# One inference step of a two-layer decoder on one core: sample latents earlier, their turnings inside an output buffer, and more unread products on TensorE

## The chip, the cores and the metric

The kernel runs on one NeuronCore of a Trainium2 chip. The metric is the device time of one launch in microseconds, the median of several runs; lower is better. TensorE (PE) multiplies matrices into PSUM, VectorE (DVE) and ScalarE (ACT) compute on what it leaves, GpSimd (POOL) and SyncE (SP) mostly issue transfers.

## The reference, cut to what matters

The program is one step of a decoder trunk with two layers, for a prompt of 512 tokens and for 8 sample requests of one token each, in float32. Layer 0 mixes tokens by sliding-window attention and retention, layer 1 by latent attention. Each layer then attends to 256 memory tokens and passes a mixture of 16 experts. The latent attention is the part in which work is moved:

```python
def mla_project(x, pos, w_in, q_norm, kv_norm, w_uq, w_uk):
    cq, ckv, kr = jnp.split(x @ w_in, [MLA_Q_RANK, MLA_Q_RANK + MLA_KV_RANK], axis=-1)
    ...
    q = (cq @ w_uq).reshape(B, S, MLA_HEADS, MLA_NOPE + MLA_ROPE)
    q_nope, q_rope = jnp.split(q, [MLA_NOPE], axis=-1)
    q_rope = rope(q_rope, pos)
    q_lat = jnp.einsum('bshn,chn->bshc', q_nope, w_uk)
```

The prompt's queries attend to 512 keys; the sample's `q_lat` and `q_rope` (8 requests, 8 heads) attend later to 1024 cached positions each, read from pages. After each memory attention a router picks two experts for each of the 520 tokens, and the tokens' rows are gathered by expert.

## The kernel before, in words

Every engine runs one program in an order written out by hand. PSUM is cut into four buffers of 1024 columns (two banks each). A list of jobs (`psum_jobs`) hands them out in turn: job n uses buffer n mod 4. `open_(key)` makes TensorE wait until job n-4, the last user of the buffer, has been released by the engine that read it; `close` tells the readers that the job is full; `taken(pe, key)` waits until a job's result has been copied out, that is for the same release. TensorE takes its instructions in order, so whatever is written behind a wait starts after it.

`unread_products(o, n)` is a helper of three lines: n float32 products of the identity with itself (128 columns) or with a constant (`routes`, 256 columns), into columns of an open buffer that nobody reads. The kernel before has 47 of them at seven places: ahead of the turning of a layer's last tile (4), around the last gated tile of retention (8 and 8), ahead of the first latent projection (6), and in the tables of the experts (2, 3, and 4 or 3).

The stages that the change touches, in order of time:

- Sliding attention. Block i is S (scores), T (the turning of the probabilities), O (the product with the values); between them stand projections of the input, `SWA_WEAVE`.
- Retention. For each tile n of 128 tokens: `retS` (scores), `retK` (keys turned), `retO` (output), `retU` (state), and the turning `retG` of the gated tile before. DVE multiplies `retS` by the decay and with that releases its buffer (line 2735).
- The state of the samples: `sU` (updates), `sO` (output), `sOt` (its turning), among the turnings `x.t` of tiles 0 to 3.
- The memory stage ends with the turnings `xm.t` of the normed tiles, the router's products `lg.t` (line 1579), and their turnings `rt` (lines 1590 and 1593). Tile 2's turning is copied by ACT alone, the others are shared by ACT (line 2109) and DVE (line 2896).
- The tables of the experts, in `experts`: `rank` (lines 1609 to 1616), `table` (1628 and 1634, twice: destinations, then gates), while DVE computes ranks and places in a chain of some fifty small instructions. DVE's line 3095 writes `block_tokens`, by which POOL gathers the rows of a block (line 883). `moeX` (line 1647) turns the gathered rows, `moeH` (1659) is the first product with an expert's weights.
- Latent attention. 16 blocks, in a software pipeline S.i+2, T.i, O.i-1 (lines 1928 and 1931; 1112; 1941). Between them stand `qn`, `qrope` (1892), `qrT` (1902, the turning of the rotary queries of a tile), `kn`, `vt` (1874, the values). Behind O.5 stand `ql` (line 1917, the sample's latents: 8 small products) and `qrT.4` (line 1905: the sample's rotary queries, 8 turnings of 8x8), each with a buffer of its own. ACT copies them out behind out.5.

Of the kernel before, what the change touches and what calls it, by code (L numbers as in the profile page):

```python
# [213 lines left out]
PAGE_DVE = keys("""pcT.0 pcT.2 pcT.4 max.0 pcT.7 scale.0 ga.2.0 ga.2.1 max.1 ga.3.0 scale.1 ga.3.1 ga.4.0 ga.4.1""")  # L214
SP_REQUESTS = 4

# [16 lines left out]
def block_order():  # L233

    out = [("X", 0), ("H", 0), ("X", 1)]
    for b in range(BLOCKS_M):
# [15 lines left out]
LATENT_BLOCKS_PE = keys("""qrope.0 kn.1 qrT.0 qn.2 qrope.1 S.0 qn.3 S.1 vt.0 qrT.1 S.2 T.0 qrope.2 S.3 T.1 O.0 vt.1 S.4 T.2 O.1 S.5 T.3 O.2  # L252
                        qrope.3 qrT.2 S.6 T.4 O.3 S.7 T.5 O.4 qrope.4 qrT.3 S.8 T.6 O.5 ql qrT.4 S.9 T.7 O.6 S.10 T.8 O.7 S.11 T.9 O.8
                        S.12 T.10 O.9 S.13 T.11 O.10 S.14 T.12 O.11 S.15 T.13 O.12 T.14 O.13 T.15 O.14 O.15""")
LATENT_BLOCKS_ACT = keys("""qn.1 kn.1 qrT.0 exp.0 qn.3 exp.1 vt.0 qrT.1 pT.0 exp.2 pT.1 out.0 exp.3 vt.1 pT.2 exp.4 out.1 pT.3 exp.5 out.2
                         qrT.2 pT.4 exp.6 out.3 pT.5 exp.7 out.4 qrT.3 pT.6 exp.8 out.5 ql qrS pT.7 exp.9 out.6 pT.8 exp.10 out.7
# [47 lines left out]
def decoder_step(nc, io, outs):  # L304
# [82 lines left out]
    with ExitStack() as ctx:  # L387
# [220 lines left out]
        def pair(key):  # L608
            return PS[:, J[key] % 4, :]
# [437 lines left out]
        def _(pe):  # L1047
# [15 lines left out]
            def transpose_x(i, t):  # L1063
# [4 lines left out]
                if i % 3 == 1 and t == NT - 1:  # L1068
                    unread_products(o[:, 896:1024], 4)
# [180 lines left out]
            def between(n):  # L1250
                for key in SWA_WEAVE[n]:
                    project(key)
# [72 lines left out]
            for n in range(4):  # L1325
# [7 lines left out]
                close(mm, key)  # L1333
                key = ("retK", n)
# [7 lines left out]
                o = open_(key)  # L1342
                taken(pe, ("retS", n))
# [50 lines left out]
            def state_output():  # L1394

                key = ("sO",)
                o = open_(key)
                taken(pe, ("sU", 3))
# [7 lines left out]
            def state_output_back():  # L1406

                key = ("sOt",)
                o = open_(key)
                taken(pe, ("sO",))  # L1410
# [42 lines left out]
            def memory_stage(l):  # L1453
# [116 lines left out]
                def logits(t):  # L1570
# [4 lines left out]
                    pe.wait_ge(s["wr_zero"], 1)  # L1575
                    taken(pe, ("xT", 3 * l + 1, t))
# [6 lines left out]
                def logits_back(t):  # L1583
                    key = ("rt", l)
                    o = open_(key) if t == 0 else pair(key)
                    if t == NT - 1:

                        taken(pe, ("xT", 3 * l + 1, t))
                        for k in range(KD):
                            pe.matmul(o[0:DB, t * 32:t * 32 + 20], xT[:, k, tile_cols(t)], wr[:, l, k, 0:20], start=(k == 0), stop=(k == KD - 1))  # L1590
                        return
                    taken(pe, ("lg", l, t))
# [11 lines left out]
            def experts(l):  # L1604
# [5 lines left out]
                unread_products(o[:, 768:1024], 2, routes)  # L1610
# [9 lines left out]
                unread_products(o[:, 768:1024], 3, routes)  # L1620
# [15 lines left out]
                block_sums(0, "dest_sums")  # L1636
                pe.wait_ge(s["dest_rows"], l + 1)
                block_table(0).then_inc(s["dest_table"], 1)
                pe.wait_ge(s["gates_ready"], l + 1)
# [40 lines left out]
                def step_x(b):  # L1680
                    key = ("moeX", l, b)
                    o = open_(key)
                    if b == 0:
                        unread_products(o[:, 768:1024], 3 if l else 4, routes)
# [3 lines left out]
                def step_h(b):  # L1688
# [4 lines left out]
                    else:  # L1693
                        pe.wait_ge(s["half_gained"], l + 1)
# [109 lines left out]
            def latent_blocks():  # L1804
# [91 lines left out]
                def q_rope_back(t):  # L1896
# [3 lines left out]
                    if t < 4:  # L1900
                        for c in range(2):
                            mm = pe.transpose(o[:, c * P:c * P + P], qr_tok[:, t % 2, c * P:c * P + P], ident[:, :])
                    else:
                        for h in range(8):
                            mm = pe.transpose(o[:, 8 * h:8 * h + 8], qr_rep[0:8, h, :], ident[0:8, 0:8])
# [29 lines left out]
                def apply(i, o, blk, v):  # L1935
                    n, h0, g, w = blk
                    taken(pe, ("vt", n // 2))
# [160 lines left out]
        def _(act):  # L2098
# [111 lines left out]
            def attention_steps(kind):  # L2210
# [19 lines left out]
                def outputs(i):  # L2230
                    n, h0, g, w = blocks[i]
                    if kind == "mla":
# [216 lines left out]
            def latent_attention():  # L2449
# [59 lines left out]
                def sample_turned():  # L2509
                    full(act, ("qrT", 4))  # L2510
                    for q in range(4):
# [855 lines left out]
```

## Time and profile before

| | us |
|---|---|
| median of 3 runs | 1015.01 (1011.78 to 1015.91) |
| the profiled execution | 1004.26 |
| its span, first to last instruction | 1002.5 |
| TensorE busy | 938.6 (94%) |
| VectorE busy | 511.1 (51%) |
| ScalarE busy | 354.1 (35%) |
| mean granted TensorE clock | 0.983 |

The profile is of one execution. "Busy" is time in which an engine ran an instruction, a share of the span. The granted clock is that of TensorE, 1.00 being 2.4 GHz and 0.50 being 1.2 GHz. In a row of the timeline, "x8" is the number of instructions that were merged, and the bracket is the idle time of the engine ahead of them and what ended it. A float32 product appears as two instructions.

### The profile page before, as it was taken

The numbers are of one execution on the slowest core, as the hardware profiler recorded it, in microseconds if no ns is written. First come the engines' busy times: TensorE is split into PE (matmuls) and PEld (weight loads), VectorE is DVE, ScalarE is ACT, GpSimd is POOL, SyncE is SP. The second block draws the span as 40 slices with busy tenths as digits, with TensorE's granted clock in tenths as the row PEclk, the third lists the DMA queues.
The fourth block names the chain that finished last, engine by engine and source line by source line (L and its number), as shares of the span: only waits on it lengthen the run. The fifth ranks groups of instructions, "written<-read, shape, count | busy, mean of one in ns | idle before, by whom it ended". The sixth has DMA issues, their size and how long they took to land.

```text
span 1002.5 us, 17774 instructions
## 1 busy us (share of the span) xinstructions
PE 938.6 (94%) x6956; PEld 570.4 (57%) x6956; DVE 511.1 (51%) x1068; ACT 354.1 (35%) x891; POOL 255.0 (25%) x307
## 2 busy tenths in 40 slices
PE   7998999999998998799999999999999979999995
PEld 6886787878544856533333666557558654333332
DVE  0236630366828758532222285775688783223237
ACT  3336442021002445133333364565215443333323
POOL 3650000051600002345420014550000025552130
PEclk9999999999999999799999999999999989999998
DMA  9827100272204472889999732460266177999977
GB/s 319 207 83 245 59 1 1 85 201 94 74 0 80 137 282 104 312 321 410 416 414 415 311 107 52 94 185 24 81 213 255 43 253 245 366 416 413 417 202 187
DMA packets 76268, 203.61 MB, mean 203 GB/s; under 512 B 18105, under 2 KB 42465, under 8 KB 67089
## 3 DMA queue, kind: packets, MB, share of 16 engines
q1 hardware_dynamic: 59264, 152.78, 41.6%
q0 software_dynamic: 16912, 49.59, 16.1%
q8 instruction: 60, 0.98, 0.4%
q14 instruction: 32, 0.25, 0.1%
HBM read 184.46 MB, written 25.92 MB: 210 GB/s over the span
## 4 chain that ended last, share of the span: by engine, by line
PE 70%; DVE 14%; DMA 9%; ACT 4%; issue 2%; POOL 1%; SPq 1%; DVEq 0%; POOLq 0%; ACTq 0%
PE PS L1659 15%; PE PS L1446 10%; PE PS L1089 8%; PE PS L1193 6%; PE PS L1676 6%; PE PS L1477 3%; DMA x<-y_tok 2%; PE PS L1647 2%; ACT arena L2100 2%; DMA ring<-in_moe_w_in_dram 2%; DMA arena<-in_moe_w_in_dram 2%; PE PS L1154 1%; PE PS L1112 1%; PE PS L1073 1%; DVE rowmax L2633 1%
## 5 line engine op out<-in xcount | busy, mean ns | idle before, releaser
L1659 PE MATMUL PS<-ring,arena 128*32 128x512 f32 x696 | 137.6, 592 | 1.0 <-DMA ring<-in_moe_w_in_dram 0.8
L2100 ACT ACTIVATE arena<-PS 32x520 f32<-32x520 f32 (+9 forms) x138 | 69.4, 515 | 161.7 <-PE PS L1089 39.3
L1659 PE MATMUL PS<-arena 128*32 128x512 f32 x600 | 106.8, 593 | 2.1 <-issue 2.1
L3182 DVE COPY arena<-PS 128x256 f32<-128x256 f32 x24 | 10.2, 425 | 174.0 <-PE PS L1667 174.0
L1089 PE MATMUL PS<-xT,ring 128*128 128x260 f32 x416 | 93.5, 385 | 4.8 <-DVE arena L2593 3.1
L1089 PEld LDWEIGHTS PS<-xT,ring 128*128 128x128 f32 x416 | 78.3, 190 | 19.1 <-DVE arena L2593 5.1
L2386 ACT ACTIVATE arena<-PS,lnc 128x128 f32<-128x128 f32 x184 | 66.9, 468 | 36.7 <-PE PS L1647 36.7
L1659 PEld LDWEIGHTS PS<-ring,arena 128*32 128x32 f32 x696 | 37.1, 110 | 55.5 <-issue 51.6
L1676 PE MATMUL PS<-ring,arena 128*32 128x512 f32 x408 | 65.4, 595 | 0.6 <-DVE arena L3182 0.6
L1193 PE MATMUL PS<-ring,xT 128*128 128x256 f32 (+2 forms) x336 | 65.2, 354 | 0.0
L887 POOL DMA_INDIRECT y_tok<-arena,slot_dest x22 | 22.3, 1014 | 167.4 <-ACT arena L2424 152.9
L849 POOL TENSOR_TENSOR rstd<-rstd,small 128x1 f32<-128x1 f32 (+1 forms) x20 | 13.5, 676 | 187.2 <-DVE rstd L2882 187.2
L1193 PEld LDWEIGHTS PS<-ring,xT 128*128 128x128 f32 (+1 forms) x336 | 57.0, 186 | 7.0 <-issue 0.2
L1446 PE MATMUL PS<-ring,xT 128*128 128x512 f32 x128 | 57.0, 593 | 0.0
L1659 PEld LDWEIGHTS PS<-arena 128*32 128x32 f32 x600 | 29.1, 110 | 47.9 <-issue 45.7
L2406 ACT ACTIVATE PS<-PS 128x256 f32<-128x256 f32 x24 | 8.8, 368 | 129.7 <-PE PS L1659 129.7
L2109 ACT ACTIVATE xT<-PS,lnc 128x128 f32<-128x128 f32 (+1 forms) x108 | 39.5, 450 | 36.9 <-PE PS L1073 19.2
L1676 PE MATMUL PS<-arena 128*32 128x512 f32 x216 | 50.8, 595 | 0.0
L2221 ACT ACTIVATE pbuf<-PS,negmax 128x256 f32<-128x256 f32 (+3 forms) x96 | 45.1, 480 | 16.1 <-DVE negmax L2640 15.9
L1659 PE MATMUL PS<-xT,arena 128*32 128x512 f32 x240 | 50.3, 592 | 0.0
L1446 PE MATMUL PS<-ring,arena 128*128 128x512 f32 x96 | 44.5, 599 | 0.5 <-DMA ring<-in_w_mem_o_dram 0.5
L1676 PE MATMUL PS<-xT,arena 128*32 128x512 f32 x144 | 43.5, 595 | 0.6 <-DVE arena L3182 0.6
(448 smaller groups left out, 1785.0 us busy)
## 6 DMA issues: line engine op xcount, KB each, us to landing
ring<-in_moe_w_in_dram SPq DMA_DIRECT2D x29, 1024.0 KB
arena<-in_moe_w_in_dram SPq DMA_DIRECT2D x25, 1024.0 KB
ring<-in_moe_w_out_dram SPq DMA_DIRECT2D x17, 1024.0 KB
ring<-in_w_in_even_dram SPq DMA_DIRECT2D x11, 1024.0 KB
xT<-in_moe_w_in_dram SPq DMA_DIRECT2D x10, 1024.0 KB
arena<-in_moe_w_out_dram SPq DMA_DIRECT2D x9, 1024.0 KB
xT<-in_moe_w_out_dram SPq DMA_DIRECT2D x6, 1024.0 KB
y_tok<-in_c_zeros_dram POOLq DMA_DIRECT2D x8, 512.0 KB, 11.2
```

Source lines behind the costliest of these rows:

```text
L887: pool.indirect_dma_start(y_tok[l][:, :], bass.IndirectOffsetOnAxis(ap=slot_dest[:, b:b + 1], axis=0), ybuf[:, buf, :], None, bounds_check ...
L1089: mm = pe.matmul(o[out_rows, 512 * h:512 * h + HALF], lhs(k), rhs(k)[:, HALF * h:HALF * h + HALF], start=(k == 0), stop=(k == nk - 1))
L1193: mm = pe.matmul(o[0:ROWS[t], n * width:n * width + width], xT[:, k, tile_cols(t)], w[:, k, cols], start=(k == 0), stop=(k == KD - 1))
L1446: mm = pe.matmul(o[0:ROWS[t], 512 * h:512 * h + 512], out_part(i, 2 * n + k, t), w[:, k, 512 * h:512 * h + 512], start=(n == 0 and k == 0) ...
L1477: mm = pe.matmul(o[:, j * r:j * r + r], w[:, k, j * P:j * P + P], xT[:, k, tile_cols(t)], start=(k == 0), stop=(k == KD - 1))
L1647: mm = pe.transpose(o[:, k * P:k * P + P], by_k[:, k, :], ident[:, :])
L1659: mm = pe.matmul(o[group(q), 0:512], xT_[:, k, group(q)], w(q, k), start=(k == 0), stop=(k == KD - 1), **quarter(q))
L1676: mm = pe.matmul(o[group(q), 512 * h:512 * h + 512], a[:, c, group(q)], w(q)[:, c, 512 * h:512 * h + 512], start=(c == 0), stop=(c == 1), ...
L2100: return act.activation(dst, src, ACT.Copy)
L2109: ins = act.activation(dst(k), src(k), ACT.Identity, scale=lnc[:, i, 0, k:k + 1], bias=lnc[:, i, 1, k:k + 1])
L2221: ins = act.activation(prob_view(kind, i)[:, h, :], score_view(kind, i)[:, h, :], ACT.Exp, bias=negmax[:, n % 2, h:h + 1], scale=SCALE[kin ...
L2386: ins = act.activation(dst[:, k, :], o[:, k * P:k * P + P], ACT.Identity, scale=lnc[:, 3 * l + 1, 0, k:k + 1], bias=lnc[:, 3 * l + 1, 1, k ...
```

## The change

Three things are done. In latent attention `ql` moves from behind O.5 to ahead of the second value product `vt.1` (on ACT: from behind out.5 to behind exp.3), and `qrT.4` loses its buffer: its eight turnings are made at the head of O.10, into the second bank of O.10's buffer, and ACT copies them with out.10. The job list is one shorter, so from `ql` on the jobs' buffers are other ones, and `vt.1` now waits for the release of S.3 where it waited for that of `qrope.2`. Third, unread products are added at these places:

| place | products added, columns | stands |
|---|---|---|
| x.1, x.2 of layer 0 | 2, 3 of 128 | behind open_, ahead of the norm's wait |
| sliding attention, ahead of qr.3 | 4 of 128 | ahead of open_ |
| retS 2 and 3 | 3, 3 of 128 | ahead of the next open_ |
| retO 0 | 5 of 128 | behind open_, ahead of taken(retS 0) |
| sO, sOt | 3, 2 of 128 | behind open_ |
| lg.1, both layers | 4 of 128 | behind open_ |
| rt, both layers | 2 of 128 | behind open_ |
| rank | 2 to 3 of 256 | ahead of the picks' wait |
| table | 3 to 6, and 1 and 1, of 256 | ahead of three waits |
| moeX 0 | 4 to 8 (layer 0), 3 to 6 (layer 1), of 256 | ahead of the gather's wait |
| moeH 0 | 1 of 256 | ahead of the gains' wait |

```diff
+TURN_UNREAD = {(0, 1): 2, (0, 2): 3, (1, NT - 1): 4, (4, NT - 1): 4}
+SAMPLE_TURNED = 10
-LATENT_BLOCKS_PE = ... T.1 O.0 vt.1 S.4 ... T.6 O.5 ql qrT.4 S.9 ...
+LATENT_BLOCKS_PE = ... T.1 O.0 ql vt.1 S.4 ... T.6 O.5 S.9 ...
-LATENT_BLOCKS_ACT = ... exp.3 vt.1 ... out.5 ql qrS pT.7 ...
+LATENT_BLOCKS_ACT = ... exp.3 ql vt.1 ... out.5 pT.7 ...
@@ transpose_x
-                if i % 3 == 1 and t == NT - 1:
-                    unread_products(o[:, 896:1024], 4)
+                unread_products(o[:, 896:1024], TURN_UNREAD.get((i, t), 0))
@@ between (sliding attention)
+                if n == 2:
+                    unread_products(pair(att_key("swa", "O", 0))[:, 896:1024], 4)
@@ retention, behind retS n
+                if n >= 2:
+                    unread_products(pair(("retG", n - 2))[:, 896:1024], 3)
@@ retO
                 o = open_(key)
+                if n == 0:
+                    unread_products(o[:, 896:1024], 5)
                 taken(pe, ("retS", n))
@@ sO
                 o = open_(key)
+                unread_products(o[:, 896:1024], 3)
                 taken(pe, ("sU", 3))
@@ sOt
                 o = open_(key)
+                unread_products(o[:, 896:1024], 2)
                 taken(pe, ("sO",))
@@ logits, logits_back
+                    if t == 1:
+                        unread_products(o[:, 896:1024], 4)
                     taken(pe, ("xT", 3 * l + 1, t))
...
+                    if t == 0:
+                        unread_products(o[:, 896:1024], 2)
                     taken(pe, ("lg", l, t))
@@ experts
-                unread_products(o[:, 768:1024], 2, routes)
+                unread_products(o[:, 768:1024], 3, routes)
                 pe.wait_ge(s["picks_ready"], l + 1)
...
-                unread_products(o[:, 768:1024], 3, routes)
+                unread_products(o[:, 768:1024], 6, routes)
...
                 block_sums(0, "dest_sums")
+                unread_products(o[:, 768:1024], 1, routes)
                 pe.wait_ge(s["dest_rows"], l + 1)
                 block_table(0).then_inc(s["dest_table"], 1)
+                unread_products(o[:, 768:1024], 1, routes)
                 pe.wait_ge(s["gates_ready"], l + 1)
...
-                        unread_products(o[:, 768:1024], 3 if l else 4, routes)
+                        unread_products(o[:, 768:1024], 6 if l else 8, routes)
                     pe.wait_ge(xs_in[b % 3], 16 * uses(BLOCKS_M, 3, l, b))
...
+                        unread_products(o[:, 768:1024], 1, routes)
                         pe.wait_ge(s["half_gained"], l + 1)
@@ apply (latent attention, TensorE)
+                    if i == SAMPLE_TURNED:
+                        pe.wait_ge(s["qrtok_ready"], NT)
+                        for h in range(8):
+                            pe.transpose(o[:, 512 + 8 * h:512 + 8 * h + 8], qr_rep[0:8, h, :], ident[0:8, 0:8])
@@ outputs (latent attention, ACT)
+                    if kind == "mla" and i == SAMPLE_TURNED:
+                        key = att_key(kind, "O", i)
+                        full(act, key)
+                        copy(oT[:, h0 // 2, tile_cols(n)], pair(key)[:, 0:P])
+                        for q in range(4):
+                            turned = pair(key)[32 * q:32 * q + 32, 512:576]
+                            ins = copy(qrS[32 * q:32 * q + 32, q, :, 0:8], turned.rearrange("p (h b) -> p b h", h=8))
+                        free(ins, key)
```

## Rows read from the trace of the kernel before

**Rows 1.** The page's chain of work that ended last, by engine.
```profile
PE 70%; DVE 14%; DMA 9%; ACT 4%; issue 2%; POOL 1%; SPq 1%; DVEq 0%; POOLq 0%; ACTq 0%
```
**Rows 2.** Windows: busy us of PE, PEld, DVE, ACT, POOL, granted clock, DMA share, GB/s.
```profile
405.20:418.90 13.70, 11.00 (x63) 7.88 (x62) 9.09 (x38) 0.87 (x4) 2.95 (x3) 0.50 0.83 292
...
687.50:695.40 7.90, 7.90 (x74) 7.81 (x72) 3.37 (x5) 4.27 (x5) 0.00 (x0) 1.00 0.01 2
```
**Rows 3.** Timeline of layer 0's router and tables: start, us, engine, line.
```profile
394.73 1.09 PE L1579 MATMUL PS<-xT,wr 128*32 128x128 f32 x32 [1.14 <-ACT xT L2109]
395.75 1.16 PE L1061 MATMUL PS<-ident 128*128 128x128 f32 x8
...
398.95 0.84 PE L1593 MATMUL PS<-small,sinf 128*128 128x20 f32 x6 [0.85 <-ACT xT L2109]
...
403.74 0.45 PE L1613 MATMUL PS<-arena,qdec 128*128 128x80 f32 x2 [1.40 <-DVE arena L3047]
...
404.84 2.43 PE L1061 MATMUL PS<-qdec,ident 128*128 128x256 f32 x6
...
408.58 1.79 PE L1628 MATMUL PS<-arena 128*32 128x128 f32 x20 [1.32 <-DVE arena L3075]
...
410.81 0.62 PE L1634 MATMUL PS<-small,arena 128*128 128x24 f32 x2 [0.43 <-ACT arena L2100]
...
411.86 0.16 DVE L3095 CAST block_tokens<-PS 128x12 uint32<-128x12 f32 x1
...
412.87 1.05 POOL L883 DMA_INDIRECT arena<-x_rows,block_tokens  x1 [12.56 <-DVE block_tokens L3095]
...
414.32 3.76 PE L1061 MATMUL PS<-qdec,ident 128*128 128x256 f32 x8
...
417.88 1.55 PE L1647 MATMUL PS<-ident,arena 128*128 128x128 f32 x8
...
424.15 0.97 PEld L1647 LDWEIGHTS PS<-ident,arena 128*128 128x128 f32 x8 [0.84 <-issue]
```
**Rows 4.** Timeline of layer 1, the first gather and what follows.
```profile
825.97 1.03 POOL L883 DMA_INDIRECT arena<-x_rows,block_tokens  x1 [12.61 <-DVE block_tokens L3095]
...
827.45 2.91 PE L1061 MATMUL PS<-qdec,ident 128*128 128x256 f32 x6
...
830.40 1.57 PEld L1647 LDWEIGHTS PS<-ident,arena 128*128 128x128 f32 x8 [0.76 <-DMA arena<-x_rows,block_tokens]
```
**Rows 5.** Timeline of retention.
```profile
212.26 1.23 DVE L2735 TENSOR_TENSOR arena<-PS,decay 128x1024 f32<-128x1024 f32 x1
213.63 1.97 PE L1346 MATMUL PS<-arena 128*128 128x64 f32 x16 [1.57 <-DVE arena L2735]
...
233.34 0.66 PE L1337 MATMUL PS<-ident,arena 128*128 128x128 f32 x4 [1.08 <-DVE arena L2778]
```
**Rows 6.** Timeline of the samples' state and the turnings of layer 0.
```profile
302.63 1.95 PE L1061 MATMUL PS<-ident 128*128 128x128 f32 x16
...
310.44 1.13 PE L1073 MATMUL PS<-ident,x 128*128 128x128 f32 x8 [1.09 <-DVE x L2888]
```
**Rows 7.** Timeline of sliding attention, ahead of qr.3.
```profile
89.21 7.28 PE L1089 MATMUL PS<-xT,ring 128*128 128x260 f32 x32 [1.87 <-DVE arena L2593]
```
**Rows 8.** Timeline of latent attention: vt.1, exp.3's end, ql, qrT.4, S.9, mask of S.14.
```profile
635.62 1.98 PE L1874 MATMUL PS<-ring,arena 128*128 128x512 f32 x4
...
636.94 0.20 ACT L2221 ACTIVATION_READ_ACCUMULATOR pbuf<-PS,negmax 128x1 f32 x1
...
653.12 1.06 PE L1917 MATMUL PS<-arena 64*128 64x8 f32 x16
...
655.02 0.66 PE L1905 MATMUL PS<-ident,arena 8*128 8x8 f32 x8 [0.83 <-ACT pbuf L2221]
655.60 0.92 PE L1928 MATMUL PS<-arena 64*128 64x384 f32 x4
...
675.06 0.43 DVE L2632 TENSOR_TENSOR PS<-PS,band 128x256 f32<-128x256 f32 x1
```

More of the change, by code:

```diff
@@ L251 @@
 LATENT_JOBS += [("oinT", 3), ("qn", 0), ("oinT", 4), ("kn", 0), ("qn", 1)]
-LATENT_BLOCKS_PE = keys("""qrope.0 kn.1 qrT.0 qn.2 qrope.1 S.0 qn.3 S.1 vt.0 qrT.1 S.2 T.0 qrope.2 S.3 T.1 O.0 vt.1 S.4 T.2 O.1 S.5 T.3 O.2
-                        qrope.3 qrT.2 S.6 T.4 O.3 S.7 T.5 O.4 qrope.4 qrT.3 S.8 T.6 O.5 ql qrT.4 S.9 T.7 O.6 S.10 T.8 O.7 S.11 T.9 O.8
+LATENT_BLOCKS_PE = keys("""qrope.0 kn.1 qrT.0 qn.2 qrope.1 S.0 qn.3 S.1 vt.0 qrT.1 S.2 T.0 qrope.2 S.3 T.1 O.0 ql vt.1 S.4 T.2 O.1 S.5 T.3 O.2
+                        qrope.3 qrT.2 S.6 T.4 O.3 S.7 T.5 O.4 qrope.4 qrT.3 S.8 T.6 O.5 S.9 T.7 O.6 S.10 T.8 O.7 S.11 T.9 O.8
                         S.12 T.10 O.9 S.13 T.11 O.10 S.14 T.12 O.11 S.15 T.13 O.12 T.14 O.13 T.15 O.14 O.15""")
-LATENT_BLOCKS_ACT = keys("""qn.1 kn.1 qrT.0 exp.0 qn.3 exp.1 vt.0 qrT.1 pT.0 exp.2 pT.1 out.0 exp.3 vt.1 pT.2 exp.4 out.1 pT.3 exp.5 out.2
-                         qrT.2 pT.4 exp.6 out.3 pT.5 exp.7 out.4 qrT.3 pT.6 exp.8 out.5 ql qrS pT.7 exp.9 out.6 pT.8 exp.10 out.7
+LATENT_BLOCKS_ACT = keys("""qn.1 kn.1 qrT.0 exp.0 qn.3 exp.1 vt.0 qrT.1 pT.0 exp.2 pT.1 out.0 exp.3 ql vt.1 pT.2 exp.4 out.1 pT.3 exp.5 out.2
+                         qrT.2 pT.4 exp.6 out.3 pT.5 exp.7 out.4 qrT.3 pT.6 exp.8 out.5 pT.7 exp.9 out.6 pT.8 exp.10 out.7
                          pT.9 exp.11 out.8 pT.10 exp.12 out.9 pT.11 exp.13 out.10 pT.12 exp.14 out.11 pT.13 exp.15 out.12 pT.14 out.13
@@ L1899, in q_rope_back @@
                     pe.wait_ge(s["qrtok_ready"], t + 1)
[L1900 to L1905, printed above, removed]
+                    for c in range(2):
+                        mm = pe.transpose(o[:, c * P:c * P + P], qr_tok[:, t % 2, c * P:c * P + P], ident[:, :])
                     close(mm, key)
@@ L2231, in outputs @@
                     n, h0, g, w = blocks[i]
-                    if kind == "mla":
+                    if kind == "mla" and i == SAMPLE_TURNED:
[6 more added lines that the diff above has]
+                        free(ins, key)
+                    elif kind == "mla":
                         take(att_key(kind, "O", i), oT[:, h0 // 2, tile_cols(n)], lambda o: o[:, 0:P])
@@ L2507, in sample_latents @@
                     free(ins, ("ql",))
-                def sample_turned():
-                    full(act, ("qrT", 4))
-                    for q in range(4):
-                        ins = copy(qrS[32 * q:32 * q + 32, q, :, 0:8], pair(("qrT", 4))[32 * q:32 * q + 32, 0:64].rearrange("p (h b) -> p b h", h=8))
-                    free(ins, ("qrT", 4))
                 exps, probs_turned, outputs = attention_steps("mla")
-                steps.update({"exp": exps, "pT": probs_turned, "out": outputs, "ql": sample_latents, "qrS": sample_turned})
+                steps.update({"exp": exps, "pT": probs_turned, "out": outputs, "ql": sample_latents})
                 for key in LATENT_BLOCKS_ACT:
```

## The prediction

> **What bounds the kernel now.** I read the chain of work that ended last first: 70% of it is TensorE, 14% DVE [rows 1]. So an instruction added to TensorE costs its whole length, unless it stands in a wait. Then I read the granted clock in windows. It is 1.00 nearly everywhere, but 0.50 (1.2 instead of 2.4 GHz) from 405.2 to 418.9 us, in the tables of layer 0, with TensorE busy 11.0 of 13.7 us [rows 2], and in a stretch as long at the same place of layer 1. TensorE had done little before either fall: in layer 0 it waited 1.40 us for the picks [rows 3]. In these stretches DVE's chain of small steps sets the pace, as the timeline shows: TensorE's waits end on DVE lines 3047 and 3075 [rows 3]. Last I read, for each place of the change, what ends the wait there, and whether the added products stand ahead of that wait or behind it.
>
> **Prices.** Eight unread products of 128 columns are busy 1.95 us [rows 6], four 1.16 [rows 3]: 0.20 us each at the full clock. Of 256 columns, four at half the clock take 3.76 [rows 3] and three 2.91 [rows 4]: 0.85 each, and 0.43 at the full clock.
>
> **The change part by part**, against the profiled execution.
>
> Sliding attention, four products ahead of the buffer wait of qr.3: 0.8 us in an idle time of 1.87 [rows 7]. Three behind retS 2 and 3, also ahead of the wait: 0.6 in 1.08 [rows 5], and the same at tile 3. Zero.
>
> retO 0, five products. They look as if they filled the 1.57 us ahead of line 1346 [rows 5]. But they stand behind `open_`, and the job list has retS 0, retK 0, two memory jobs, retO 0: the buffer that retO 0 opens is retS 0's, and is released by the same DVE instruction (line 2735) for which `taken` waits. The wait is over when they start. What follows is TensorE and DVE in turn (line 1346, the state, its copy on DVE, the next tile), with no slack: 5 x 0.20 = +1.0 us. Bounds: 0 if something unseen were late as well, 1.2 at the price of the row with four.
>
> Samples' state. sO is the same trap: its buffer is sU 3's, for which it also waits. Three products behind that wait, then three ahead of x.2's norm, make 1.2 us, of which the idle time of 1.09 ahead of x.2 [rows 6] hides all but +0.1. The two of sOt and the two of x.1 lie in waits of their own. Bounds: 0, and 2.0 if all ten were on the path.
>
> lg.1, both layers. Its idle time of 1.14 ends with ACT line 2109 [rows 3], the copy of tile 2's turning, which frees the very buffer that lg.1 opens. The four products come behind it, 0.8 us. They push the four products and the turning of tile 4 by about 0.5, but what is waited for next (398.95, again ACT's copies, of tile 3) does not depend on them: I take 0, at most 0.4 a layer. rt, both layers: its buffer is freed by that last copy too, so its two products (0.4) come after the wait of 0.85 [rows 3], and the router's turnings, DVE's whole chain and the gather behind them start 0.4 later. That is +0.4 in each layer, counted in the next part.
>
> Tables, if the clock stays up. The third rank product (0.43) fits in the 1.40 ahead of the picks. The table's six (2.6 us, from 404.84+0.4) end at 407.8, ahead of the places (408.58+0.4). The one before L1634 (0.43) lies in a wait of 0.43; line 3095, which releases the gather, comes at its turn on DVE, which is busy till then. So the gather starts at 412.87+0.4 [rows 3]. In layer 1 it took 830.40-825.97 = 4.43 us to the turning that waited for it [rows 4]; in layer 0 this gives 417.3, and 417.7 after. Before, TensorE was still busy with the four slow products and turned at 417.88 [rows 3]. Eight at the full clock are 3.4 us from about 414.0: 417.4, in time. The turnings of the first half take 0.3 less (weight loads 1.57 at half the clock [rows 4], 0.97 at the full [rows 3], half of the difference). Layer 0: -0.2-0.3 = -0.5, rt's 0.4 inside. Layer 1 waited for the gather before, so +0.4-0.3 = +0.1. The product ahead of moeH (0.43) lies in a wait of about 1 us.
>
> Latent attention. Behind O.5, ql takes TensorE from 653.12, then qrT.4 waits 0.83 us for exp.8, turns, and S.9 starts at 655.60 [rows 8]. Without both S.9 could start at 653.1: -2.5. But ahead of vt.1 (635.62) ql costs its 1.0, and vt.1's buffer is now S.3's, released when exp.3 has ended, at 636.94+0.20 = 637.14 [rows 8]: vt.1 starts at 637.2, +1.6 in all (ql hides in it). All that follows to S.8 hangs on S and exp by turns, so S.9 gains 2.5-1.6 = 0.9. T.7 then waits some 0.2 for exp.8. The eight turnings in O.10 (0.6, [rows 8]) meet DVE, which takes S.14's mask at 675.06, half a us after its scores end: +0.1. ACT has the four copies in its wait for T.12. Together -0.6. Bounds: -1.6 if vt.1 didn't wait, +0.6 if nothing at S.9 came back.
>
> Sum: +1.0 +0.1 -0.5 +0.1 -0.6 = +0.1 us. The profiled execution took 1004.26 (span 1002.5 and 1.8 around it), the median of the runs is 1015.01, 10.8 above it. No step of the sum depends on what makes that difference, so I carry the +0.1 over: 1015.1.
>
> **The rule weighed against the trace.** From 687.5 to 695.4 TensorE ran turnings, nearly all 64 of them without a gap, and the clock stayed 1.00 [rows 2]. The Trainium skill, "TensorE: Matmul & The Clock Gate", section "Part 4: PE-mode transpose", says that a transpose does not count as activity for the clock. By that rule the turnings ahead of moeH would not bring it back; by the row they do. The row decides.
>
> **Rivals.**
> (a) The clock falls in spite of the products. Then the table's six take 5.1 us, end at 410.4, 1.4 after the places; the product before L1634 costs 0.85 instead of 0.43; the gather leaves 1.1 later than with the clock up; and the eight ahead of moeX run from 416.2, slow till 418.9 and fast from there, to 420.9 where 417.88 was: +3.1-0.3 = +2.8 in layer 0. Layer 1 with six, by the same steps, +2.5. With the rest: +1.1-0.6+5.3 = +5.8, 1020.8. It decides at the products behind 404.84: as soon as those start slow. For it: the stretch of the tables has few real products. Against it: the stretch before the fall now holds three products more, and rt's are moved into it.
> (b) The low clock costs half its length. If all work in the two low stretches were on TensorE's path, half of its busy 11.0 us would come back, twice: -11, and 1004. Against it: DVE is busy 9.1 of those 13.7 us [rows 2], and TensorE's waits end on it. The skill's page named above, section "Terms", counts the penalty as throttled time x (1-K/N), which is 13.7 us for the two stretches and would give 1001; the rows on DVE speak against it.
> (c) The timed executions lie 10.8 us above the profiled one, and a part of that may be low clock at waits where this execution kept it, in retention or the router, with long product runs behind. If the products at those waits hold it, -6: 1009. Nothing in this trace shows it; only the distance speaks for it.
> (d) The products behind waits are all on the path: 5+10 in layer 0's first half, 6 and 6 around the routers, 27 x 0.20 = 5.4, where the sum has 1.9; with latent attention at its upper bound (+0.6) and the tables as forecast without rt's part (-1.2) that is +4.8: 1020.
> (e) The change does nothing: the clock falls as before, with the long waits hiding all the products. 1015.
>
> **How the numbers follow.** About 0.5% (5 us) is what a measurement of this kernel tells from no change. Forecast 0.52, (a) 0.14, (b) 0.07, (c) 0.14, (d) 0.07, (e) 0.06. Slower by over 0.5%: most of (a) and (d), 0.18. Faster: (b) and most of (c), 0.20. The rest, 0.62, is within. The likeliest case alone has 1012 to 1018; the range reaches 1009 of (c) and 1020.8 of (a): 1008 to 1021.
>
> **What would show it.** After: a granted clock of 1.00 through both tables (wrong: 0.50 there, with the six products at 0.85 each). Line 1346 of tile 0 about 1.1 us behind DVE's line 2735 instead of 0.1. rt's two products between ACT's copy and line 1593, with 0.4 us more. moeX 0 of layer 0 waiting for the gather. vt.1 with an idle time ended by ACT, S.9 right behind O.5. The prediction is wrong if the clock falls in the tables, if the gain of latent attention is above 1.6 or below zero, or if the span moves by more than 5 us.

## The result and the profile after

| | before | after |
|---|---|---|
| median, us | 1012.31 (10 runs, 1006.43 to 1017.01) | 1007.21 (10 runs, 1002.71 to 1009.71) |
| ratio, 95% interval | | 0.9944 (0.9921 to 0.9967) |
| profiled execution, us (span) | 1004.26 (1002.5) | 1005.44 (1003.7) |
| mean granted clock of it | 0.983 | 0.994 |

The change is worth 0.56%, where no move was forecast. The ratios, here and below, are of fast executions alone. Against the forecast of 1015.1 the median is 7.9 us lower, of which 2.7 are the base: the kernel before has a median of 1012.31 over these ten runs, where the three runs of the prediction had 1015.01. The two profiled executions say the opposite: the one of after is 1.2 us longer. That is no contradiction, but the point of this case. The profiled execution of before, on which the whole prediction rests, was one of its luckiest: of 104 further executions of that kernel three took 1004.3 or less, and their mean was 1013.1.

First, the two profiles against each other. The busy line and the chain of after:

```profile
PE 951.3 (95%) x7072; PEld 580.4 (58%) x7072; DVE 511.1 (51%) x1068; ACT 354.0 (35%) x891; POOL 254.8 (25%) x307
...
PE 74%; DVE 12%; ACT 6%; DMA 5%; issue 2%; POOL 1%; SPq 0%; DVEq 0%; POOLq 0%; ACTq 0%
```

TensorE's share of the chain has grown from 70% [rows 1], and the unread products of 128 columns (line 1063) are now among its lines, with 1%. Windows of after (length, then busy us of PE, PEld, DVE, ACT, POOL with counts, granted clock, DMA share, GB/s): the tables of layer 0, the stretch at vt.1, the stretch behind O.5, and one at 705 us.

```profile
399.00:418.00 19.00, 15.93 (x140) 12.46 (x140) 14.99 (x65) 2.88 (x11) 5.04 (x7) 1.00 0.86 302
637.20:640.60 3.40, 3.40 (x7) 0.84 (x5) 0.00 (x0) 1.01 (x1) 2.14 (x4) 0.50 0.43 99
...
656.00:680.00 24.00, 23.87 (x172) 12.51 (x168) 19.05 (x44) 15.99 (x45) 11.28 (x21) 1.00 0.59 195
705.40:708.90 3.50, 3.50 (x53) 2.32 (x48) 1.14 (x1) 0.00 (x0) 0.00 (x0) 0.51 0.00 0
```

The tables keep 1.00 where they had 0.50 [rows 2]. Two short stretches at 0.50 are new against the first profile, at vt.1 and at 705 us.

Retention, TensorE of after (start, us, engine, line; the bracket is the idle time ahead and what ended it). The wait of 1.48 ends with DVE's line 2753 (2735 before), and only then do the five products run. Line 1353 (1346 before) starts 1.2 us behind its old place [rows 5]:

```profile
213.71 1.38 PE L1063 MATMUL PS<-ident 128*128 128x128 f32 x10 [1.48 <-DVE arena L2753]
214.93 1.90 PE L1353 MATMUL PS<-arena 128*128 128x64 f32 x16
```

The router and the tables of layer 0, same columns. The six products of the table take 2.79 and end ahead of the places. The eight ahead of moeX 0 take 3.70 and the turnings (line 1662, 1647 before) start 0.5 later than before [rows 3]. But this execution came 0.8 late to lg.1 (395.50 against 394.73) and lost 0.55 more at rt (400.27 against 398.95, less those 0.8). It is 1.3 late there and 0.5 late at the turnings, so the tables gave back 0.8. lg.1's own four products took 1.1; the wait of 0.85 that stood ahead of rt, now gone, hides them:

```profile
395.50 1.16 PE L1063 MATMUL PS<-ident 128*128 128x128 f32 x8 [1.12 <-ACT xT L2125]
396.59 1.09 PE L1590 MATMUL PS<-xT,wr 128*32 128x128 f32 x32
...
399.73 0.71 PE L1063 MATMUL PS<-ident 128*128 128x128 f32 x4
400.27 0.74 PE L1606 MATMUL PS<-small,sinf 128*128 128x20 f32 x6
...
406.07 2.79 PE L1063 MATMUL PS<-qdec,ident 128*128 128x256 f32 x12
409.81 1.36 PE L1641 MATMUL PS<-arena 128*32 128x128 f32 x20 [0.95 <-DVE arena L3093]
...
414.70 3.70 PE L1063 MATMUL PS<-qdec,ident 128*128 128x256 f32 x16
418.39 1.16 PE L1662 MATMUL PS<-ident,arena 128*128 128x128 f32 x8
```

Latent attention, TensorE of after: ql (line 1929), a wait of 0.52 for exp.3 as worked out, then vt.1, which takes 3.10 instead of 1.98 [rows 8] as the clock falls under it; further on, S.9 (line 1940) right behind the work of O.5, where ql, the wait and qrT.4 stood:

```profile
634.87 1.06 PE L1929 MATMUL PS<-arena 64*128 64x8 f32 x16
636.45 3.10 PE L1890 MATMUL PS<-ring,arena 128*128 128x512 f32 x4 [0.52 <-ACT pbuf L2237]
639.48 1.22 PE L1940 MATMUL PS<-arena 64*128 64x256 f32 x4
...
654.97 0.66 PE L1957 MATMUL PS<-pT,xT 128*64 128x128 f32 x8
655.56 0.92 PE L1940 MATMUL PS<-arena 64*128 64x384 f32 x4
```

Every local step is there, and the span moved by 1.2 us where 0.1 was forecast. So the 5 us must come from executions that look different. The theory that the experiments test, the **clock theory** (rival (c), widened): in other executions of the kernel before the clock falls in more places, with work behind them that TensorE bounds, and the change prevents that. Its rival, the **order theory**: the gain is the new order of the work (the wait behind O.5 gone), and the profiled pair hides it by chance. In the texts recorded before the first four runs they are called theory 1 and theory 2; theory 3 there is that transfers make the executions differ.

### The profile page after: what moved, and what is told of

Its sections match the earlier page's. It is cut to its first block, busy times and chain, and to the rows that moved or that the text cites. A ratio compares the mean times of both kernels' runs of the same rounds, so it can differ in the third digit from the quotient of the medians.

```text
span 1003.7 us, 17995 instructions
## 1 busy us (share of the span) xinstructions
PE 951.3 (95%) x7072; PEld 580.4 (58%) x7072; DVE 511.1 (51%) x1068; ACT 354.0 (35%) x891; POOL 254.8 (25%) x307
## 4 chain that ended last, share of the span: by engine, by line
PE 74%; DVE 12%; ACT 6%; DMA 5%; issue 2%; POOL 1%; SPq 0%; DVEq 0%; POOLq 0%; ACTq 0%
PE PS L1674 16%; PE PS L1455 10%; PE PS L1090 8%; PE PS L1691 8%; PE PS L1194 6%; PE PS L1486 3%; DMA x<-y_tok 2%; PE PS L1662 2%; ACT arena L2116 2%; PE PS L1113 2%; PE PS L1155 1%; PE PS L1063 1%; ACT xT L2125 1%; PE PS L1074 1%; DMA ring<-in_w_in_even_dram 1%
## 5 line engine op out<-in xcount | busy, mean ns | idle before, releaser
L3200 DVE COPY arena<-PS 128x256 f32<-128x256 f32 x24 | 10.2, 425 | 172.9 <-PE PS L1682 172.9
```

## The experiments

Each timed kernel ran 12 times. They ran in three groups (the first four, the next four, the last four of the table), each with its own 34 or 35 runs of the kernel before. "Clock lost" is (1 - mean granted clock) x span, averaged over the runs: the full-speed time that the low clock took away, if all of it were on the path. It is not: in each of the 18 profiles 2.3 to 4.0 us of it stand behind the last product, where TensorE has nothing left to do (the window below is the end of before's first profile). The ratio stands with its 95% interval; it is not the quotient of the two medians of all runs. Beside it stands the ratio of the plain means of the same executions.

```profile
995.80:1002.50 6.70, 0.00 (x0) 0.00 (x0) 4.10 (x7) 1.54 (x3) 0.00 (x0) 0.50 0.40 157
```

| kernel | median, us | range | ratio | by means | clock lost, us |
|---|---|---|---|---|---|
| before, all three groups | 1013.2 | 1002.5 to 1023.2 | | | 28.9 |
| b_again (before, unedited) | 1014.50 | 1006.8 to 1020.5 | 0.9997 (0.9961 to 1.0032) | 1.0004 | 29.8 |
| products_only | 1011.40 | 1006.9 to 1015.7 | 0.9970 (0.9941 to 0.9999) | 0.9984 | 11.5 |
| move_only | 1009.01 | 1003.9 to 1018.2 | 0.9934 (0.9897 to 0.9972) | 0.9960 | 24.9 |
| tables_only | 1011.33 | 1005.6 to 1018.0 | 0.9988 (0.9953 to 1.0024) | 0.9988 | 17.0 |
| turn_only | 1010.30 | 1007.6 to 1018.9 | 0.9984 (0.9956 to 1.0012) | 0.9984 | 27.6 |
| ql_only | 1013.83 | 1006.6 to 1022.2 | 1.0007 (0.9977 to 1.0037) | 0.9999 | 29.1 |
| turn_filled | 1009.02 | 1006.4 to 1018.2 | 0.9979 (0.9951 to 1.0007) | 0.9973 | 24.0 |
| front_only | 1013.06 | 1009.1 to 1023.0 | 1.0022 (0.9991 to 1.0053) | 1.0005 | 26.7 |
| after_again (the changed kernel) | 1006.07 | 1002.6 to 1009.8 | 0.9960 (0.9927 to 0.9992) | 0.9948 | 7.3 |
| freed | 1005.38 | 1001.6 to 1010.0 | 0.9942 (0.9913 to 0.9971) | 0.9936 | 6.3 |
| freed_vt | 1004.22 | 1000.3 to 1006.8 | 0.9918 (0.9890 to 0.9947) | 0.9918 | 5.7 |
| move_vt | 1006.70 | 1002.9 to 1014.4 | 0.9966 (0.9935 to 0.9997) | 0.9960 | 22.6 |

(One run of before at 5371 us and one of turn_filled at 3317 us are left out.) Over the 104 runs of before, an execution's time rises by 0.91 us with each us of clock lost, from 986.9 at none (correlation 0.91). What makes executions of this kernel differ goes with the clock; theory 3, by which the clock would be the same in all of them, falls with that. The line is not one for other kernels: after_again lost 7.3 us of clock, where it reads 993.5, and its mean was 1006.5.

### Where the low clock lies: six profiles of the kernel before

The unedited kernel was run once more in the first group, and four times later for its profile alone.

> The kernel before, once more, without any edit. Theory 1 (the gain of the change is low clock avoided: the one profiled execution of before, 1004.3, was its fastest, and its typical execution, 1012, loses more to a low clock): its executions spread over some 10 us, and their mean granted clock falls as their time rises, from about 0.983 at 1004 to about 0.975 at 1014. Theory 2 (the gain is the order of the work in latent attention) and theory 3 (the spread is transfers): the clock is 0.983 in all of them, whatever the time. The ratio to before should be 1.000, which also shows how well five rounds tell kernels apart.

> The kernel before, unedited; this run and the next three are for their profiles. Fixed places: low clock recurs at 214 to 225 us (price 4.2) and behind O.5, 655 to 679 us (price 5 to 7), each in 1 to 3 of the four, and always in both tables; an execution's time is 1004.3 plus the prices of its stretches, to 2 us. Spread loss: low stretches elsewhere, outside those two places and the tables, make up more than half of the time above 1004.3.

> As before_1: tables low; retention and O.5 low or not, with 4.2 and 5 to 7 us where low.

> As before_1: tables low; retention and O.5 low or not, with 4.2 and 5 to 7 us where low.

> As before_1: tables low; retention and O.5 low or not, with 4.2 and 5 to 7 us where low.

b_again's executions spread over 14 us, with the clock falling faster than I expected: about 0.970 at 1014 us, where I had 0.975. Its profiled execution took 1020.23, 16 us more than the one the prediction used, with the same instructions in the same order. Two of its low stretches, as windows:

```profile
214.40:224.60 10.20, 10.20 (x45) 9.30 (x45) 5.48 (x9) 0.00 (x0) 5.05 (x8) 0.50 1.04 214
...
664.90:678.60 13.70, 13.53 (x56) 6.80 (x56) 4.75 (x12) 5.41 (x21) 8.24 (x17) 0.50 0.45 101
```

In both TensorE is busy nearly all the time and DVE 54% and 35% of it: here TensorE sets the pace, which it did not in the tables [rows 2]. The second begins behind ql, the wait and the turnings of qrT.4. TensorE of b_again:

```profile
663.18 1.06 PE L1917 MATMUL PS<-arena 64*128 64x8 f32 x16
665.07 1.02 PE L1905 MATMUL PS<-ident,arena 8*128 8x8 f32 x8 [0.83 <-ACT pbuf L2221]
666.02 1.65 PE L1928 MATMUL PS<-arena 64*128 64x384 f32 x4
```

The same four instructions of S.9 took 0.92 in [rows 8].

To see what each stretch costs, I matched DVE's instructions of two profiles one by one and took how far one runs behind the other at fixed points. The differences from point to point (points in us of before's first profile, rounded; the last column closes the sum to the span) give the time gained or lost in each section against that first profile:

| profile (span) | to 203 | retention, to 232 | samples' state, memory attention, to 380 | router, tables, to 440 | experts, to 600 | latent, to 680 | to 850 | to the end |
|---|---|---|---|---|---|---|---|---|
| b_again (1018.5) | 0.0 | +4.2 | +2.1 | +1.0 | +2.9 | +5.9 | +1.8 | -1.8 |
| before_1 (1009.9) | -0.1 | +1.4 | +2.0 | +0.2 | -0.8 | +4.4 | +1.1 | -0.7 |
| before_2 (1009.7) | +1.9 | +4.2 | +0.2 | 0.0 | -0.9 | +2.9 | +0.5 | -1.7 |
| before_3 (1008.3) | +1.8 | 0.0 | 0.0 | 0.0 | -0.7 | +2.9 | +2.0 | -0.2 |
| before_4 (1005.8) | +0.3 | 0.0 | +1.1 | -0.8 | -0.4 | +1.3 | +1.8 | 0.0 |
| **mean of the six of before** (the first counts as 0) | +0.7 | +1.6 | +0.9 | +0.1 | 0.0 | +2.9 | +1.2 | -0.7 |
| after (1003.7) | +0.2 | +1.2 | -0.6 | -0.7 | -0.9 | +1.0 | +3.1 | -2.2 |
| after_again (1002.1) | +0.1 | +1.2 | -0.6 | -0.6 | -0.1 | -0.6 | +2.0 | -1.8 |
| **mean of the two** | +0.1 | +1.2 | -0.6 | -0.6 | -0.5 | +0.2 | +2.6 | -2.0 |

Of the section of latent attention, the length of the low stretch behind O.5 explains nearly all: it was 13.7 us long in b_again, 10.2 in before_1, 6.9 in before_2 and before_3, 3.4 in before_4, none in the first profile, and cost 5.9, 4.4, 2.9, 2.9, 1.3 and 0: about 0.42 us for each us. before_1 to before_4 ran on one and the same chip. Windows of before_2, retention, the tables, and behind O.5:

```profile
216.90:227.10 10.20, 10.20 (x43) 9.00 (x43) 5.68 (x10) 0.00 (x0) 5.27 (x8) 0.50 1.05 223
411.50:425.10 13.60, 11.03 (x63) 7.88 (x62) 9.11 (x38) 0.87 (x4) 2.95 (x3) 0.50 0.83 294
660.60:667.50 6.90, 6.90 (x32) 3.62 (x31) 2.37 (x6) 2.80 (x12) 4.02 (x9) 0.51 0.44 96
```

Five of six profiles have a low stretch behind O.5 (all of the four where I expected one to three), at prices from 1.3 to 5.9 where I expected 5 to 7. In retention, 10.2 us of low clock cost 4.2 in two of six, and 6.8 us cost 1.4 in a third. The tables were low in all six. So the fixed places recur, with lengths that differ. That an execution's time follows from its stretches at these two places to 2 us held for before_1, 2 and 4, not for before_3 and b_again: retention and latent attention together give 10.1 of 16.0, 5.8 of 7.5, 7.1 of 7.2, 2.9 of 5.9 and 1.3 of 3.3 us. Two more places recur. A low stretch of 3.4 us at 313 to 317 us (b_again, before_4) cost 1.6, and one at 706 to 708 us (before_3, before_4) cost 1.8.

The last rows sum to +6.6 for before and +0.4 for after, and the difference, 6.2 us, is near the 5.1 between the medians (two profiles of after are few). It comes from latent attention (-2.7), the part from the samples' state to memory attention (-1.5), the tables (-0.7), the start and the experts (-1.0), retention (-0.4), and the two sections behind 680 cancel (+1.4 and -1.3).

The +1.4 comes from the place at 705 us: both profiles of after have a low stretch of 3.4 us there, at a price of 2.3 to 2.4. Over all 18 profiles it stands in six of the seven of kernels with added products at the front or in the tables, and in two of the eleven others. This count was made after the fact, and no run shows why, but it is a cost that no step of the prediction had. What moves the last section was not traced.

### The two halves of the change

products_only takes the move back, move_only takes all added products out; tables_only is the kernel before with the products of the tables, moeX and moeH alone (the edits in short):

```
products_only:  T.6 O.5 S.9              ->  T.6 O.5 ql qrT.4 S.9       (and qrT.4's buffer, qrS)
move_only:      - unread_products(...)       at every place of the table of the change
tables_only:    + unread_products(o[:, 768:1024], 3 / 6 / 1 / 1 / 8 (6) / 1, routes)   and nothing else
```

> All added unread products, but ql and qrT.4 where they were before. Theory 1: all of the gain, 5 to 7 us (ratio 0.993 to 0.995), clock 0.994 or more. Theory 2: 1 to 3 us slower than before (ratio 1.001 to 1.003), since retO's five products and rt's two cost 1.8 us.

> ql ahead of vt.1 and the sample's turnings inside O.10, no product added. Theory 1: no gain, ratio 0.999 to 1.002; the new wait ahead of vt.1 (0.5 us, behind ql's small products) may let the clock fall there, as it did in the profile of the changed kernel. Theory 2: ratio 0.994.

> Only the products in rank, table, moeX 0 and moeH 0 are added. Theory 1 in its narrow form (the two tables are where the clock falls): nearly all of the gain, 4 to 6 us, since without rt's and retO's products nothing is paid for it. Theory 1 in its wide form (retention, the samples' state and the routers lose the clock too in other executions): 1 to 3 us of the gain (ratio 0.997 to 0.999), clock about 0.988. Theory 2: 0 to 1 us, the 0.5 + 0.3 us worked out in the prediction.

The move gives the larger part of the whole, though its forecast was -0.6 us; move_only and move_vt, each over its own runs of before and taken together, have a ratio of means of 0.9960 (0.9942 to 0.9977), 4.1 us. That is what the order theory expected of move_only (0.994), and not the clock theory, which had looked for the low clock at the products alone; the next runs ask what in the move pays. The products alone read 0.9970 or, by the means, 0.9984, hardly told from none, and lie between the two expectations. And **the clock that they save is not the time that they save**: tables_only loses 12 us less than before and is 1.2 us faster by either ratio, though its interval reaches from 4.8 us faster to 2.4 slower; products_only loses 18 us less and is 1.6 to 3 us faster. The profile of tables_only says the same: from 380 to 440 us it gains 0.8 on before's first profile, and 0.5 at the tables of layer 1. That is the reading of [rows 2], that DVE sets the pace in the tables, borne out. In the table above the whole section gains 0.7 from it, rt's late start included.

### What in the move pays

turn_only moves the turnings alone, ql_only moves ql alone, turn_filled moves nothing and fills the wait, front_only has only the products of sliding attention, retention and the samples' state (the edits in short):

```
turn_only:    T.6 O.5 ql qrT.4 S.9   ->  T.6 O.5 ql S.9        (turnings in O.10)
ql_only:      O.0 vt.1 ... O.5 ql qrT.4  ->  O.0 ql vt.1 ... O.5 qrT.4
turn_filled:  + if t == 4:
              +     unread_products(pair(("mlaO", 5))[:, 896:1024], 4)
                o = open_(("qrT", 4))
front_only:   + the products of sliding attention, retS, retO, x.1, x.2, sO, sOt
```

> The kernel before with one edit: the samples' eight turnings go from their own buffer behind ql into the output buffer of block 10. ql stays behind O.5, vt.1 keeps its place, no products are added. Order theory (the gain of the move is its place in the queue): the 0.83 us wait of qrT.4 and its turnings, about 1.5 us, leave the path: ratio 0.998 to 0.999. Clock theory (what costs is the clock that falls behind ql and the wait, and stays half for some 14 us of work that TensorE bounds, in part of the executions): with the wait gone it falls seldom there: ratio 0.994 to 0.996, and the full-speed time lost (one minus the mean granted clock, times the span) falls from 29 us by about 5. In the profile no low stretch between 655 and 680.

> The kernel before with one edit: ql goes ahead of vt.1; the turnings of the samples stay behind O.5 in their own buffer with their wait. No products are added. Order theory: S.4 starts 1.6 later and S.9 gains 1.0 back: ratio 1.000 to 1.001. Clock theory: the stretch behind O.5 has 1.0 us less of the eight-column products but keeps the wait, and a new stretch of ql with a wait stands ahead of vt.1: it loses about as often as before: ratio 0.998 to 1.002. If it reads below 0.996, ql's place is what pays in the move.

> The kernel before with one addition: four unread products of 128 columns (0.8 us) ahead of the buffer wait of qrT.4, behind ql. Nothing is moved. Order theory: they lie in the wait of 0.83 us: ratio 1.000. Clock theory: the clock is held there in most executions: ratio 0.994 to 0.997, and 4 to 8 us less of full-speed time lost.

> The kernel before with the unread products of sliding attention, retention and the samples' state alone (no products at the routers and tables, nothing moved). Sum by the order of the work: retO 1.2 us later, samples' state 0.1: ratio 1.001. Clock theory: the executions whose clock was low at 214 to 225 us and 316 to 320 us lose 3 to 6 us less there: mean ratio 0.997 to 0.999, with the full-speed time lost lower by 3 to 6 us. If the products alone gained through the tables, this one reads 1.000 to 1.002.

turn_only showed an error common to both of my theories: its wait does not go. TensorE of turn_only:

```profile
655.39 1.06 PE L1914 MATMUL PS<-arena 64*128 64x8 f32 x16
657.29 1.23 PE L1925 MATMUL PS<-arena 64*128 64x384 f32 x4 [0.83 <-ACT pbuf L2222]
658.45 1.65 PE L1928 MATMUL PS<-arena 32*128 32x384 f32 x4
```

Now S.9 waits the same 0.83 for exp.8, since it opens the buffer that qrT.4 had opened, and the clock falls behind ql as before, for 17 us:

```profile
657.80:674.80 17.00, 17.00 (x70) 8.62 (x68) 7.25 (x18) 6.21 (x18) 10.40 (x20) 0.50 0.56 152
```

That stretch cost 7.4 us, again 0.43 for each us. ql_only, with a wait behind O.5 as well (1.23 us, ahead of S.9), equals before. Only both together shift S.9's and T.7's turn so that no wait follows O.5: in all six profiles with both (after, after_again, freed, freed_vt, move_only, move_vt) there is no low stretch there; of the eleven profiles of kernels that keep either there and fill nothing, nine have one (not the first profile of before, nor ql_only's). In turn_filled the products run where the wait was, and qrT.4 and S.9 follow at full speed:

```profile
657.45 1.06 PE L1919 MATMUL PS<-arena 64*128 64x8 f32 x16
658.45 1.16 PE L1061 MATMUL PS<-ident 128*128 128x128 f32 x8
659.53 0.66 PE L1907 MATMUL PS<-ident,arena 8*128 8x8 f32 x8
660.12 0.92 PE L1930 MATMUL PS<-arena 64*128 64x384 f32 x4
```

Its ratio, 0.9979, lies between the two expectations and its interval reaches 1.0007; its median is 4.4 us under before's and it lost 5.5 us less clock. It speaks for the clock theory without deciding by itself. Together with the nil of ql_only and the table of sections it does: in latent attention the move gives -0.4 to -0.6 by its order (after_again -0.6, freed -0.6, freed_vt -0.4, move_vt -0.4: the four of the six in which the clock held at vt.1), and most of the rest of its gain is the stretch that no longer comes, 2.9 us on average. The two make 3.4 of the 4.1 us.

front_only lost only 2 to 3 us less clock and gained nothing (expected 0.997 to 0.999). What the products can save in retention (1.6 on average over the six profiles) the five at retO nearly take back (1.2 in every profile that has them). In the section behind it the samples' products seem to help: of the twelve profiles without them six have a low stretch between 232 and 380 us, of the six with them none.

### The changed kernel mended

freed takes four of the groups that stood behind a buffer wait (at retO, sO, lg.1 and rt) and places them ahead of it, in a half of a buffer that nobody reads then; freed_vt fills vt.1's new wait as well; move_vt is the move with that filling alone (the edits in short, two lines in one):

```
freed:      - o = open_(("retO", n)); if n == 0: unread_products(o[:, 896:1024], 5)
            + if n == 0: unread_products(pair(("retK", 0))[:, 896:1024], 5); o = open_(("retO", n))
            (sO's 3 into retG 3's, lg.1's 4 into lg.0's, rt's 2, now 3, into lg.2's, in the same way)
freed_vt:   + if i == 1: unread_products(pair(("mlaO", 0))[:, 896:1024], 3)
              o = open_(("vt", i))
```

> The changed kernel, unedited, in the same call as its variants: ratio 0.993 to 0.996 by the runs so far, full-speed time lost about 7 us. If the wide gain is low clock avoided, no execution of it lies above 1011 and the profile has no low stretch in retention (214 to 225 us) or behind O.5.

> The changed kernel with its products that stood behind a buffer wait moved ahead of it, each into a buffer that is free in that half: retO 0's five, sO's three, lg.1's four and rt's two (three here). By the wait-then-products reading 1.2 us at retO and 0.55 at each rt come back: 2 us faster than the changed kernel, ratio 0.991 to 0.993; line 1346's turn 0.1 us behind DVE's line 2737. If those products cost nothing on the path, it equals the changed kernel.

> freed, and three unread products of 128 columns (0.6 us) ahead of the buffer wait of vt.1, to fill the idle time behind ql. If the low stretch at 637 to 641 us of the changed kernel is caused by ql and that idle time, it goes and gives 1 to 2 us more: ratio 0.989 to 0.992. If it is only where the execution happened to be looked at, equal to freed.

> The move alone with the same three products ahead of vt.1; no other products. Against the move alone (0.9934, 0.990 to 0.997): if the fall at vt.1 costs as it did in that profile (3.7 us for the four products of vt.1 where the full clock takes 1.9), ratio 0.991 to 0.993. If no fall there, 0.993 to 0.995.

after_again did as expected: no execution above 1009.8, and no low stretch behind O.5 or from 214 to 225 us. But retention was not free of it; a short one came just ahead, with TensorE busy throughout, and its section lost no more than after's:

```profile
209.10:212.50 3.40, 3.40 (x20) 3.18 (x17) 3.33 (x3) 0.63 (x2) 3.40 (x7) 0.50 1.02 396
```

TensorE of freed in retention: the products fill the wait, and line 1353 starts when DVE's product with the decay (line 2753) is done.

```profile
212.24 1.28 PE L1063 MATMUL PS<-ident 128*128 128x128 f32 x10
213.98 1.97 PE L1353 MATMUL PS<-arena 128*128 128x64 f32 x16 [0.46 <-DVE arena L2753]
```

Its section of retention reads 0.0 where after has +1.2. By means over the 12 runs freed is 0.9988 (0.9968 to 1.0008) of after_again: 1.2 us where 2 were expected, not told from zero by the times alone, though the profile shows the 1.2. Against before it reads 0.9942, short of the 0.991 to 0.993 expected. freed_vt is 0.9970 (0.9952 to 0.9988) of after_again and the fastest kernel of all, 1004.2: 3.0 us by the means. Against before it reads 0.9918, as expected. Its vt.1 waits for nothing and keeps the clock:

```profile
635.03 1.06 PE L1931 MATMUL PS<-arena 64*128 64x8 f32 x16
636.02 0.94 PE L1063 MATMUL PS<-ident 128*128 128x128 f32 x6
636.80 1.88 PE L1892 MATMUL PS<-ring,arena 128*128 128x512 f32 x4
```

In move_only, where nothing was filled, the two products of vt.1 (four instructions) took 3.68 at the low clock, and the section lost 1.5 against the profiles without that fall; after had it too, after_again and freed not. No section shows the fall at vt.1 in the two kernels that fill it, but it was absent in two of the five without (after_again, freed; present in after, move_only, ql_only), and move_vt, which fills vt.1 and nothing else, reads the same 0.9960 by the means as move_only, where 0.991 to 0.995 was expected. So that filling vt.1 gains time is not shown.

## Why the prediction was wrong

**The step that failed** is the last of the sum: "No step of the sum depends on what makes that difference, so I carry the +0.1 over." Against the mean of the 104 runs the profiled execution was 8.8 us fast, and that distance goes with the low clock, most of all behind O.5, a place that the change touches. It was visible as a question: the profile was 7.5 us under the fastest of the three timed runs shown. Rival (c) said so and priced it at -6 (1009); the runs gave -5.1. That the size came so near is partly luck: (c) placed the low clock in retention or the router and had the products hold it, while the larger part lay behind O.5 and went with the move. There the sum had the order of the work alone, -0.6; the runs gave -4.1, of which 2.9 were low clock that no term and no rival had. I gave (c) 0.14 because nothing in the one trace showed it. The trace could not show it. The distance could.

**The ranking of the low stretches** failed with it. I took the two stretches that I saw, in the tables, for the clock question of this kernel. They are the cheap ones: the products took some 14 us of half clock out of layer 0's, and the section gained 0.7 us, or 1.2 with rt's 0.55 added back, as DVE paces it. The dear ones were not in the trace: behind O.5 at some 0.42 us for each us, in retention at 0.41 (4.2 for 10.2) or 0.20 (1.4 for 6.8).

**The local terms** mostly held, against the same first profile. retO: +1.2, forecast +1.0; the buffer trap was read rightly. Samples' state: +0.1 forecast, and no section of the six variants with those products lost anything. Sliding attention: nothing, as forecast. Router and tables of layer 0: clock 1.00 throughout in after and after_again, -0.6 to -0.7, forecast -0.5; lg.1's four products were hidden, as taken, and rt's two cost 0.55 instead of 0.4. Router and tables of layer 1, from 800 to 850 us: +0.7 in after and -0.3 in after_again, forecast +0.1; rt's two products cost 0.4 there in both, as forecast. Latent attention: -0.4 to -0.6 where the clock held at vt.1, forecast -0.6, with vt.1 waiting for exp.3 and S.9 behind O.5 as worked out; where it fell there, +1.0, which no step had. Of the signs that I named for a wrong prediction, a fall in the tables and a span moved by more than 5 us did not show in the profiled pair. The third did: the gain of latent attention was below zero, as the section lost 1.0, by the fall at vt.1. It pointed at the clock in latent attention, though not at the place that pays; a pair of single executions could not show that one.

**The rivals.** (a) and (e) fell: in none of the six profiles with the tables' products did the clock fall as before in the tables. tables_only has 3.4 us of it in each layer, at 402 and 822 us; freed_vt has 3.4 in the router of layer 0, freed in that of layer 1, and the other three none. (b) fell by tables_only: 12 us less clock lost, 1.2 us gained. The Trainium skill, "TensorE: Matmul & The Clock Gate", section "Terms", gives the penalty as throttled time x (1-K/N), K/N being the share of the clock that is granted. By it the 14 us at half clock in layer 0 cost 7 us, an estimate; 0.7 to 1.2 came back, so the profiles do not agree there. Behind O.5 its 0.5 for each us is near the 0.42 measured. The measurement decides. TensorE paces the one stretch and DVE the other, as their busy shares show. (d) fell: 1.2 at retO, 0.55 and 0.4 at the two routers, not 5.4.

**The rule on turnings.** The row from 687.5 to 695.4 us [rows 2] shows that turnings kept a clock that was already at 1.00. The prediction read it as if it showed that they bring a low clock back; it does not show that, and no run was made for it.

**What stays open.** Why an execution's clock falls at O.5 for 3.4 us, 13.7 us or not at all is not known from these runs. By the ratios with intervals the halves do not add up well: 0.9934 and 0.9970 would give 0.990, the whole reads 0.9944, within the intervals. By the means they do: 0.9960 and 0.9984 give 0.9944, and the whole reads 0.9948 in after_again. The gain of 1.5 between 232 and 380 us rests on six profiles against two. Of it, 0.9 are low stretches that after does not have; the other 0.6 stands as well in profiles of kernels without its products (before_4, tables_only, ql_only, turn_filled, move_vt). Why the low stretch at 705 us comes with the products is open.

## What to carry to other kernels

Set the profiled execution against the timed runs before summing anything: if it lies under all of them, its trace may lack the very stretches that a change might remove, and more profiles of the unedited kernel come ahead of any working. A low clock costs what the pacing engine makes it cost: look at whether TensorE is busy all the time in the stretch and how busy DVE is, and rank stretches by that ahead of length. A filler product belongs ahead of the buffer wait, in a bank that nobody reads; behind `open_` it starts when the wait is over and costs its full length, as at retO and rt, unless another wait hides it, as at lg.1.

## What the hardware showed that was not expected

The same program took 1002.5 to 1020.3 us on one chip, within one group (1002.5 to 1023.2 over three groups on three chips), and 82% of the variance of the 104 runs goes with the granted clock (0.91 us for each us lost). Between 3.4 and 17 us of half clock followed a piece of only 1.06 us of eight-column products and 0.83 us of waiting behind O.5, in nine of the ten profiles that have both; with four products in that wait the clock stayed at full speed in the one profile taken. An instruction-by-instruction match of two profiles of one program gives the price of a stretch to a few tenths of a us: 5.9 for 13.7, 4.4 for 10.2, 2.9 for 6.9 twice, 1.3 for 3.4, 7.4 for 17.0.
